# Softmax attentions with a fused bias-and-minimum instruction, row sums from a column of ones, and heads weighted together

## The chip, the cores and the metric

The kernel runs on one core of one Trainium2 chip. The metric is the device time of one execution of the whole program in microseconds; less is better.

## The reference

The program is one long network: three blocks of dense and attention layers over 256 positions of width 1024, all in fp32. The change touches only its softmax attentions, of which there are five: three branches of a sparse attention with 16 heads (two on causal rows, one on 15 compressed positions), a forgetting attention with 16 heads, and a block attention with 8 heads.

```python
# first_block, nsa: three branches share q; gates is a sigmoid per head and branch
s = einsum('qghd,ngd->ghqn', qi, kcb) - slopes * dist_c       # compressed, 15 positions
p_cmp = masked_softmax(s, dist_c >= 0, -1)
o_cmp = einsum('ghqn,ngd->qghd', p_cmp, vcb)
...                                                           # o_sel, o_win: the same on the causal rows
o = gb[..., 0:1] * o_cmp + gb[..., 1:2] * o_sel + gb[..., 2:3] * o_win

# second_block, fox_mix: forgetting attention
log_f = log_sigmoid(fz + fgate_b)
c = cumsum(log_f, axis=1)
logits = q @ k.T * FOX_HD ** -0.5 + c[q] - c[k]
probs = softmax(where(pos_q >= pos_k, logits, -inf))
out = probs @ v

# third_block, moba_attention: with 256 positions one causal block
p = softmax(where(mask, q @ k.T * dh ** -0.5, -1e30))
out = p @ v
```

## The kernel before, in words

The 256 positions are two tiles (`t`, `TT = 2`) of 128 partitions. The program is a list of stages. Each stage has a part for each engine, and unless a stage is "open" all four engines meet at a barrier at its end (`Chip.phase_end`: drain, increment `phase_done`, wait for all four). Dense stages (`SplitWeights` and what derives from it) stream weights from a ring of four 1 MB slots, split each half into a high and a low part (ScalarE L1116, VectorE L1124), and do three products for one. Attention stages use no weights.

A causal attention is made by `causal_attention` (L2402) as three stages:

- `Scores` (L2285). One job per tile and head: the product of 128 queries with the `n` keys that they can see (`n` is 128 for tile 0, 256 for tile 1) into one of four PSUM banks; VectorE adds the bias (`how`: distance times slope at L3565, decay and mask at L3523, scale and mask at L3689) and writes `p`; then `row_max` (L2331) takes the negated maximum of the row; ScalarE does the exponential with this as bias, in place, and its accumulator gives the row sum (L2350). TensorE waits for the bias instruction of four jobs ago before it fills a bank again. When all are done, VectorE waits for ScalarE's drain (L2351) and takes the reciprocals of the sums (L2344). In the compressed branch 32 multiplications with a mask come before that (L2343).
- `Gates` (L2520), in the sparse attention only: two small products of the reciprocals with the gates of the branch, in a stage of their own.
- `Turn` (L1532): transposes of `p` on TensorE, four to a bank, copied out by VectorE (L1566) and ScalarE (L1573) in turn.
- `Values` (L2354): products of the transposed weights with the values, 8 heads of 64 columns to a bank; VectorE scales each head by its own factor into `h_tok` (L2387), or scales and adds (L2385) in the second and the compressed branch. 8 or 16 heads of a tile are 8 or 16 instructions.

In the order of the program: projections, the causal branches 1 and 2, `Compress` (a small network on the keys and values), the compressed branch, then `Features` and `OutProj`. In the forgetting attention `ToNormedHeads` projects and norms, `ForgetGates.add_up` makes the cumulated decays `c` and `c_t` with five small products, `ToHeads` (L2539) brings queries and keys to feature order, and in it GpSimd issues 16 DMAs (L2563) that write one row of decays into each head's keys; `Scores` begins with a wait for them (`decays_landed`). The order in each engine is that of the program; nothing is planned by cost.

## Time and profile before

| | |
|---|---|
| median of 3 runs | 3816.76 us (3811.96 to 3827.05) |
| profiled execution | 3812.13 us, span 3810.3 us |
| TensorE busy | 3637.0 us (95%) |
| VectorE busy | 3061.5 us (80%) |
| ScalarE busy | 2060.6 us (54%) |
| GpSimd busy | 122.1 us (3%) |
| DMA | 744.52 MB, mean 195 GB/s |

Durations below come from the profiled execution. A duration in a timeline row runs from start to end of an instruction, and neighbours on one engine overlap, so the pace of an engine is read from start to start. "Idle before" says how long the engine stood and what ended it. A matrix product of fp32 operands shows as two rows. "ACTq", "DVEq" and "POOLq" are the queues of ScalarE, VectorE and GpSimd, as a barrier or a DMA issued there shows.

### The profile page before, as it was taken

To read this page: it belongs to the slowest core of one execution; us is meant where nothing else is said; L and a number is where in the kernel's file an instruction comes from. 1 tells how busy PE (TensorE), PEld (TensorE's weight loads), DVE (VectorE), ACT (ScalarE), POOL (GpSimd) and SP (SyncE) were. 2 spreads that over 40 slices of the span, in tenths; PEclk is the share of its full clock that TensorE was granted. 3 is DMA by queue.
4 is the path that set the end of the run, shared out by engine and by line. 5 is a ranking of instruction groups with operands and counts; after the bars stand their busy time and mean duration, and the time that the engine had idled before them with its cause. 6 is when DMAs were issued, how large, how long until landed. Compare 5 with 4: busy or idle time off the path is not lost. (4 is left out here: it accounts for less than half of the span.)

```text
span 3810.3 us, 59916 instructions
## 1 busy us (share of the span) xinstructions
PE 3637.0 (95%) x22328; PEld 3116.2 (82%) x22328; DVE 3061.5 (80%) x6382; ACT 2060.6 (54%) x4449; POOL 122.1 (3%) x112
## 2 busy tenths in 40 slices
PE   6999999999889979999999999999999999999898
PEld 5887788887778767998888887799988888888687
DVE  7887688887678776988888956689798997788766
ACT  3554555555355545545656456554555655555455
POOL 0000000000000000400000000050000000000000
PEclk9999999999789989999999999999999999999899
DMA  8767375766247523544454454254455545686354
GB/s 325 277 243 287 125 295 209 299 221 240 100 181 268 213 85 138 184 156 177 178 185 180 166 188 156 78 177 159 174 177 179 181 172 178 232 308 261 122 188 155
DMA packets 119619, 744.52 MB, mean 195 GB/s; under 512 B 13857, under 2 KB 14273, under 8 KB 44833
## 3 DMA queue, kind: packets, MB, share of 16 engines
q1 hardware_dynamic: 118082, 737.57, 52.9%
q8 instruction: 178, 2.92, 0.3%
q10 hardware_dynamic: 416, 2.06, 0.1%
q0 software_dynamic: 832, 1.06, 0.1%
q14 instruction: 111, 0.91, 0.1%
HBM read 738.53 MB, written 1.05 MB: 194 GB/s over the span
## 5 line engine op out<-in xcount | busy, mean ns | idle before, releaser
L212 PE MATMUL bank<-h_split,weights_high 128*128 128x512 f32 (+1 forms) x5824 | 1714.7, 358 | 15.5 <-DVE h_split L723 9.4
L1116 ACT ACTIVATE weights_high<-weight_ring 128x512 fp32r<-128x512 f32 x2248 | 1292.6, 624 | 650.9 <-PE bank L212 377.1
L1124 DVE TENSOR_TENSOR weights_low<-weight_ring,weights_high 128x512 fp32r<-128x512 f32 x2168 | 1394.9, 687 | 274.5 <-ACT weights_high L1116 252.9
L212 PE MATMUL bank<-h_split,weights_low 128*128 128x256 f32 x4800 | 1269.2, 280 | 0.0
L212 PEld LDWEIGHTS bank<-h_split,weights_high 128*128 128x128 f32 x5824 | 1014.8, 189 | 163.4 <-issue 16.7
L212 PEld LDWEIGHTS bank<-h_split,weights_low 128*128 128x128 f32 x4800 | 911.1, 190 | 37.8
L212 PE MATMUL acc<-weights_high,hidden_high 128*128 128x512 f32 x1552 | 613.8, 395 | 2.6 <-DVE hidden_low L1298 2.4
L212 PE MATMUL acc<-weights_high,hidden_low 128*128 128x512 f32 x1552 | 605.0, 390 | 0.0
L212 PE MATMUL acc<-weights_low,hidden_high 128*128 128x512 f32 x1552 | 604.5, 390 | 0.0
L212 PEld LDWEIGHTS acc<-weights_high,hidden_low 128*128 128x128 f32 x1552 | 291.3, 188 | 63.9
L212 PEld LDWEIGHTS acc<-weights_low,hidden_high 128*128 128x128 f32 x1552 | 291.7, 188 | 59.8 <-issue 0.2
L212 PEld LDWEIGHTS acc<-weights_high,hidden_high 128*128 128x128 f32 x1552 | 291.3, 188 | 56.2 <-issue 4.2
L1263 ACT ACTIVATE work<-bank 128x256 f32<-128x256 f32 x264 | 101.8, 386 | 344.9 <-PE bank L212 344.9
L212 PE MATMUL bank<-weights_high,h_split 128*128 128x512 f32 x704 | 222.8, 395 | 7.4 <-DVEq L234 2.9
L212 PEld LDWEIGHTS bank<-weights_high,h_split 128*128 128x128 f32 x704 | 133.6, 190 | 38.8 <-DVEq L234 3.9
L2249 DVE TENSOR_TENSOR h_tok<-h_feat,work 128x2048 f16<-128x2048 f16 x128 | 156.0, 1219 | 0.0
L2169 ACT ACTIVATE work<-bank 128x256 f32<-128x256 f32 x128 | 49.2, 384 | 193.2 <-PE bank L212 193.2
L212 PE MATMUL bank<-work 128*128 128x64 f32 (+10 forms) x896 | 125.6, 333 | 19.5 <-ACTq L234 8.3
L212 PE MATMUL bank<-weights_low,h_split 128*128 128x512 f32 x352 | 138.3, 393 | 0.0
L212 PEld LDWEIGHTS bank<-work 128*128 128x128 f32 (+5 forms) x896 | 108.0, 213 | 35.4 <-ACTq L234 11.1
L2171 ACT ACTIVATE work<-bank 128x256 f32<-128x256 f32 x128 | 49.3, 385 | 141.2 <-PE bank L212 141.2
L348 DVE SCALAR_TENSOR_TENSOR mod_sums<-h_tok,columns,mod_sums 128x512 f32<-128x512 f32 x160 | 112.5, 746 | 15.5 <-DMA h_tok<-slots 14.8
(347 smaller groups left out, 3522.1 us busy)
## 6 DMA issues: line engine op xcount, KB each, us to landing
weight_ring<-stream SPq DMA_DIRECT2D x574, 1024.0 KB, 4.8
h_feat<-slots SPq DMA_DIRECT2D x96, 512.0 KB, 5.8
h_tok<-slots SPq DMA_DIRECT2D x94, 512.0 KB, 5.9
work<-slots SPq DMA_DIRECT2D x26, 512.0 KB, 8.4
mod_sums<-biases SPq DMA_DIRECT2D x7, 1536.0 KB
h_feat<-rows SPq DMA_DIRECT2D x8, 512.0 KB, 3.8
work<-rows SPq DMA_DIRECT2D x7, 512.0 KB, 4.7
work<-biases SPq DMA_DIRECT2D x1, 1536.0 KB
```

The costliest lines, as they stand in the source:

```text
L212: ins = self.nc.tensor.matmul(out, lhs, rhs, start=start, stop=stop)
L348: ins = dve.scalar_tensor_tensor(self.sums.where[:, a], k.buffers[self.buffer][:, h * BANK:(h + 1) * BANK], c, self.sums.where[:, a], ALU. ...
L1116: act.activation(k.w_hi[:, b, q * self.QUARTER:(q + 1) * self.QUARTER], self.raw(g, q), ACT.Copy).then_inc(k.highs_ready, 1)
L1124: return eng.tensor_tensor(k.w_lo[:, b, w], self.raw(g, q), k.w_hi[:, b, w].bitcast(F32), ALU.subtract)
L1263: act.activation(self.rests[:, part, :], self.bank_of(c, part)[:, S:2 * S], ACT.Copy).then_inc(k.scalar_for_vector.sem, k.scalar_for_vecto ...
L2169: act.activation(self.place(c), k.bank[:, c % 2, 0:S], ACT.Gelu).then_inc(k.hidden_made, 1)
L2171: act.activation(self.place(c), k.bank[:, c % 2, S:2 * S], ACT.Copy).then_inc(k.hidden_rests, 1)
L2249: dve.tensor_tensor(cut(hot2), grid(self.places, N_KEYS), spread(self.pairs[:, S + b * BATCH:S + (b + 1) * BATCH, :], N_KEYS), ALU.is_equal)
```

## The change

- In `Scores` VectorE does one `tensor_tensor_reduce` per job: `p = (scores + bias) * scale` with a negative scale, and the minimum of `p` over the row into `low`. Sign and slope move into the constants and the scale; for the sparse attention the slope is divided out of the queries beforehand (`steep`, a factor for each feature column instead of a number). ScalarE takes the exponential of `-p + low` without an accumulator. A dummy exponential stands at the head of ScalarE's part.
- The values have a 65th column of ones for each head (`VW`), written by GpSimd in the first `Scores`, so that the product in `Values` also gives the row sum. Keys with a mask of the compressed branch are set to zero by two multiplications in place of 32.
- `Values` fills banks with at most 7 heads of 65 columns (16 heads: 5, 5 and 6), takes the reciprocals of the sums, multiplies them with the gates (where there are gates; the stage `Gates` is gone) and weights all heads of a bank in one instruction with a broadcast factor. In the second and the compressed branch the result goes to `parts` and GpSimd adds it to `h_tok`. All fills have a bank of their own, in `bank` and `acc`.
- In the forgetting attention the decay of the query row, the same for a whole row of scores, is no longer added; three of the five small products in `add_up` and one copy go. GpSimd issues the 16 DMAs of the key decays in `ToNormedHeads` (`hand_out`), when VectorE has made them and ScalarE has cleared the places, and no more in `ToHeads`.

The core of the diff (the rest: semaphores, the copies into 65-wide places, and the passing of arguments):

```diff
-    out["dist"] = np.where(tok >= q[None, None, :], tok - q[None, None, :], 1e32).reshape(P, -1)
+    out["dist"] = np.where(tok >= q[None, None, :], q[None, None, :] - tok, -1e32).reshape(P, -1)
...
-    out["cmp_dist"] = np.where(d >= 0, d, 1e32).reshape(P, -1)
+    out["cmp_dist"] = np.where(d >= 0, -d, -1e32).reshape(P, -1)
     out["cmp_mask"] = (d >= 0).reshape(P, -1)
+    out["steep"] = HD ** -0.5 / nsa_slope(2 * np.arange(DC)[None, :] + p[:, None] // HD)
...
@@ -2292,6 +2312,8 @@
 
     def gpsimd(self, pool):
         k = self.k
+        if self.ones is not None:
...
@@ -2306,9 +2328,10 @@
 
 
 
-    def __init__(self, k, jobs, top, total, keep=None, decays=0):
+    def __init__(self, k, jobs, low, keep=(), decays=0, ones=None):
         super().__init__(k)
-        self.jobs, self.top, self.total, self.keep, self.decays = jobs, top, total, keep, decays
+        self.jobs, self.low, self.keep, self.decays, self.ones = jobs, low, keep, decays, ones
+        self.scored = k.scored.reserve(len(jobs))
 
     def tensor(self, pe):
         k = self.k
@@ -2316,77 +2339,93 @@
             pe.wait_ge(k.decays_landed, 16 * self.decays)
         for i, (product, n, how, p) in enumerate(self.jobs):
             if i >= NB:
-                pe.wait_ge(k.vector_for_tensor.sem, k.vector_for_tensor.take())
+                pe.wait_ge(k.scored.sem, self.scored + i - NB + 1)
             product(k.bank[:, i % NB, 0:n]).then_inc(k.banks_for_vector.sem, k.banks_for_vector.send())
-        k.vector_for_tensor.skip(NB)
 
     def vector(self, dve):
         k = self.k
-        n_jobs = len(self.jobs)
-        begun = []
-
-        def row_max(i):
-            n, p = self.jobs[i][1], self.jobs[i][3]
-            dve.wait_ge(k.vector_for_tensor.sem, begun[i])
-            dve.tensor_reduce(self.top[:, i:i + 1], p, AX, ALU.max, negate=True).then_inc(k.vector_for_scalar.sem, k.vector_for_scalar.send())
-
+        for i, (product, n, (bias, scale), p) in enumerate(self.jobs):
+            dve.wait_ge(k.banks_for_vector.sem, k.banks_for_vector.take())
+            dve.tensor_tensor_reduce(p, k.bank[:, i % NB, 0:n], bias, scale, 3e38, ALU.add, ALU.min,
+                                     accum_out=self.low[:, i:i + 1]).then_inc(k.scored.sem, 1)
+        for p, keep in self.keep:
+            dve.wait_ge(k.scalar_for_vector.sem, k.scalar_for_vector.take())
+            dve.tensor_tensor(p, p, keep, ALU.mult)
+
+    def scalar(self, act):
+        k = self.k
+        act.activation(k.small[:, 88:89], k.small[:, ONES:ONES + 1], ACT.Exp)
+        per = len(self.jobs) // max(1, len(self.keep))
         for i, (product, n, how, p) in enumerate(self.jobs):
+            act.wait_ge(k.scored.sem, self.scored + i + 1)
+            ins = act.activation(p, p, ACT.Exp, scale=-1.0, bias=self.low[:, i:i + 1])
+            if self.keep and i % per == per - 1:
+                ins.then_inc(k.scalar_for_vector.sem, k.scalar_for_vector.send())
+
+
+class Values(Stage):
+
+
+
+    def __init__(self, k, heads, jobs, out, total, gates=None, parts=None, floor=False):
+        super().__init__(k)
+        self.heads, self.jobs, self.out, self.total = heads, jobs, out, total
+        self.gates, self.parts, self.floor = gates, parts, floor
+        n = -(-heads // (BANK // VW))
+        cuts = [heads * i // n for i in range(n + 1)]
+        self.fills = [(t, a, b) for t in range(TT) for a, b in zip(cuts, cuts[1:])]
+        self.weighted = k.weighted.reserve(len(self.fills)) if parts is not None else None
+
+    def bank(self, f):
+        return self.k.bank[:, f, :] if f < NB else self.k.acc[:, f - NB, :]
+
+    def tensor(self, pe):
+        k = self.k
+        for f, (t, a, b) in enumerate(self.fills):
+            for h in range(a, b):
+                p_t, v = self.jobs[t * self.heads + h]
+                for i, (lhs, rhs) in enumerate(zip(p_t, v)):
+                    mm = k.mm(self.bank(f)[:, (h - a) * VW:(h - a + 1) * VW], lhs, rhs, start=i == 0,
+                              stop=i == len(v) - 1, last=True)
+            mm.then_inc(k.banks_for_vector.sem, k.banks_for_vector.send())
+
+    def result(self, f):
+        t, a, b = self.fills[f]
+        return self.out[:, t, a * HD:b * HD].rearrange("p (h d) -> p h d", d=HD)
+
+    def part(self, f):
+        t, a, b = self.fills[f]
+        at = (t * self.heads + a) * HD
+        return self.parts[:, at:at + (b - a) * HD].rearrange("p (h d) -> p h d", d=HD)
+
+    def vector(self, dve):
+        k = self.k
+        for f, (t, a, b) in enumerate(self.fills):
             dve.wait_ge(k.banks_for_vector.sem, k.banks_for_vector.take())
-            how(dve, p, k.bank[:, i % NB, 0:n]).then_inc(k.vector_for_tensor.sem, k.vector_for_tensor.send())
-            begun.append(k.vector_for_tensor.sent)
-            if i >= 1:
-                row_max(i - 1)
-        row_max(n_jobs - 1)
-        dve.wait_ge(k.scalar_for_vector.sem, k.scalar_for_vector.take())
-        if self.keep is not None:
-            for i, (product, n, how, p) in enumerate(self.jobs):
-                ins = dve.tensor_tensor(p, p, self.keep(i), ALU.mult)
-        dve.reciprocal(self.total[:, 0:n_jobs], self.total[:, 0:n_jobs])
-
-    def scalar(self, act):
-        k = self.k
-        for i, (product, n, how, p) in enumerate(self.jobs):
-            act.wait_ge(k.vector_for_scalar.sem, k.vector_for_scalar.take())
-            act.activation(p, p, ACT.Exp, bias=self.top[:, i:i + 1], accum_out=self.total[:, i:i + 1])
-        act.drain().then_inc(k.scalar_for_vector.sem, k.scalar_for_vector.send())
-
-
-class Values(Stage):
-
-
-
-    def __init__(self, k, jobs, add, width=64):
-        super().__init__(k)
-        self.jobs, self.add, self.w = jobs, add, width
-        self.per = BANK // width
-
-    def tensor(self, pe):
-        k = self.k
-        for i, (p_t, v, factor, out) in enumerate(self.jobs):
-            f, j = i // self.per, i % self.per
-            if j == 0 and f >= NB:
-                pe.wait_ge(k.vector_for_tensor.sem, k.vector_for_tensor.take())
-            for a, (lhs, rhs) in enumerate(zip(p_t, v)):
-                mm = k.mm(k.bank[:, f % NB, j * self.w:(j + 1) * self.w], lhs, rhs, start=a == 0,
-                          stop=a == len(v) - 1, last=True)
-            if j == self.per - 1:
-                mm.then_inc(k.banks_for_vector.sem, k.banks_for_vector.send())
-        fills = len(self.jobs) // self.per
-        k.vector_for_tensor.skip(min(NB, fills))
-
-    def vector(self, dve):
-        k = self.k
-        for i, (p_t, v, factor, out) in enumerate(self.jobs):
-            f, j = i // self.per, i % self.per
-            if j == 0:
-                dve.wait_ge(k.banks_for_vector.sem, k.banks_for_vector.take())
-            src = k.bank[:, f % NB, j * self.w:(j + 1) * self.w]
-            if self.add:
-                ins = dve.scalar_tensor_tensor(out, src, factor, out, ALU.mult, ALU.add)
-            else:
-                ins = dve.tensor_scalar(out, src, factor, None, ALU.mult)
-            if j == self.per - 1:
-                ins.then_inc(k.vector_for_tensor.sem, k.vector_for_tensor.send())
+            src = self.bank(f)[:, 0:(b - a) * VW].rearrange("p (h d) -> p h d", d=VW)
+            total = self.total[:, t * self.heads + a:t * self.heads + b]
+            sums = src[:, :, HD]
+            if self.floor:
+                dve.tensor_scalar(total, sums, 0.5, None, ALU.max).then_inc(k.dve_step, 1)
+                dve.wait_ge(k.dve_step, k.step("dve"))
+                sums = total
+            dve.reciprocal(total, sums).then_inc(k.dve_step, 1)
+            dve.wait_ge(k.dve_step, k.step("dve"))
+            if self.gates is not None:
+                dve.tensor_tensor(total, total, self.gates[:, t, a:b], ALU.mult).then_inc(k.dve_step, 1)
+                dve.wait_ge(k.dve_step, k.step("dve"))
+            dst = self.result(f) if self.parts is None else self.part(f)
+            ins = dve.tensor_tensor(dst, src[:, :, 0:HD], total.unsqueeze(2).to_broadcast([P, b - a, HD]), ALU.mult)
+            if self.parts is not None:
+                ins.then_inc(k.weighted.sem, 1)
+
+    def gpsimd(self, pool):
+        k = self.k
+        if self.parts is None:
+            return
+        for f in range(len(self.fills)):
+            pool.wait_ge(k.weighted.sem, self.weighted + f + 1)
+            pool.tensor_tensor(self.result(f), self.result(f), self.part(f), ALU.add)
 
 
 def weight_blocks(p0, p1, heads):
...
@@ -2556,13 +2578,6 @@
                 ins = eng.tensor_copy(dst, half) if parity == 0 else eng.activation(dst, half, ACT.Copy)
             ins.then_inc(sent.sem, sent.send())
 
-    def gpsimd(self, pool):
-        k = self.k
-        for h in range(FOX_HEADS):
-            key = self.dst[HD:HD + 1, DC + h // 2, :] if h % 2 == 0 else self.odd[1][0:1, h // 2, :]
-            pool.dma_start(key, self.decays[h:h + 1, :]).then_inc(k.decays_landed, 16)
-
-
 class ToNormedHeads(ToTokens):
 
...
-            for a in range(t + 1):
-                k.mm(k.acc[:, 3, t * H:(t + 1) * H], tri[:, a, t * P:(t + 1) * P], self.lf[:, a, :],
-                     start=a == 0, stop=a == t, last=True)
         for a in range(TT):
             mm = k.mm(k.acc[0:H, 2, 0:S], self.lf[:, a, :], tri[:, a, :], start=a == 0, stop=a == TT - 1, last=True)
         mm.then_inc(k.banks_for_vector.sem, k.banks_for_vector.send())
...
+            dve.tensor_scalar(self.c_t, k.acc[0:H, 2, 0:S], -1.0, None, ALU.mult).then_inc(k.decays_made, 1)
+
+    def hand_out(self, pool):
+
+        k = self.k
+        pool.wait_ge(k.decays_made, 1)
+        pool.wait_ge(k.heads_cleared, 2)
+        for h in range(FOX_HEADS):
+            key = self.even[HD:HD + 1, DC + h // 2, :] if h % 2 == 0 else self.odd[1][0:1, h // 2, :]
+            pool.dma_start(key, self.c_t[h:h + 1, :]).then_inc(k.decays_landed, 16)
 
     def fill(self, act, dst, value):
         n, rows = dst.shape[0], dst.rearrange("p c (t q) -> p (c t) q", q=P)
...
 
     def how(t, h, n):
-        return lambda dve, dst, bank: dve.scalar_tensor_tensor(dst, bank, c[:, t, h:h + 1], mask[:, t, 0:n],
-                                                               ALU.add, ALU.add)
-
-    att = causal_attention(k, FOX_HEADS, side(0), side(DC), lambda h, a: v[:, a, h * HD:(h + 1) * HD], how, p, p_t,
-                           top, total, total, k.h_tok, False, decays=FOX_HEADS)
+        return mask[:, t, 0:n], -1.0
+
+    att = causal_attention(k, FOX_HEADS, side(0), side(DC), lambda h, a: v[:, a, h, :], how, p, p_t, low, total,
+                           k.h_tok, decays=FOX_HEADS, ones=v[:, :, :, HD])
     return out + att + [Features(k, k.h_tok), OutProj(k)]
 
...
+    projected = ToTokens(k, [(v[:, :, :, 0:HD], None)])
+    parts, branches = p.rearrange("p a b -> p (a b)"), gates.rearrange("p t (h b) -> p t h b", b=3)
     out = [head, features, projected]
     for branch in (1, 2):
         first = DC + 4 + 4 * (branch - 1)
         kt = lambda h, first=first: feat[64 * (h % 2):64 * (h % 2) + 64, first + h // 4, :]
-        val = lambda h, a, b=branch: v[:, a, (b - 1) * kv + h // 4 * HD:(b - 1) * kv + (h // 4 + 1) * HD]
-        att = causal_attention(k, H, q, kt, val, alibi(dist), p, p_t, top, total, factor, k.h_tok, branch == 2)
+        val = lambda h, a, b=branch: v[:, a, (b - 1) * NSA_GROUPS + h // 4, :]
+        att = causal_attention(k, H, q, kt, val, alibi(dist), p, p_t, low, total, k.h_tok,
+                               ones=v[:, :, :, HD] if branch == 1 else None, gates=branches[:, :, :, branch],
+                               parts=parts if branch == 2 else None)
         if branch == 1:
             att[0].copy_couples(feat[:, DC:DC + 4, :], couples)
-        out += [att[0], Gates(k, factor, gates, total, branch), att[1], att[2]]
```

## Rows read from the trace of the kernel before

**Rows 1.** Timeline of TensorE, sparse attention: start us, us, engine, line, operation, count, idle before.

```profile
931.46 0.71 PE L212 MATMUL bank<-work 64*128 64x128 f32 x8 [0.72 <-ACTq L234]
...
950.62 7.74 PE L1549 MATMUL bank<-constants,work 128*128 128x128 f32 x48 [3.68 <-DVEq L234]
959.08 10.93 PE L212 MATMUL bank<-work 128*128 128x64 f32 x96 [0.72 <-ACTq L234]
...
971.77 0.72 PE L212 MATMUL bank<-work 64*128 64x128 f32 x8 [1.76 <-DVEq L234]
...
990.93 8.06 PE L1549 MATMUL bank<-constants,work 128*128 128x128 f32 x48 [3.68 <-DVEq L234]
...
1039.14 7.34 PE L212 MATMUL bank<-work 64*128 64x15 f32 x64 [0.53 <-DVEq L234]
1054.56 5.20 PE L1549 MATMUL bank<-constants,work 128*15 128x128 f32 x32 [8.07 <-DVEq L234]
```

**Rows 2.** Timeline of TensorE, forgetting attention, from its scores to its transposes.

```profile
2379.29 0.79 PE L212 MATMUL bank<-work 65*128 65x128 f32 x2 [4.94 <-POOLq L234]
...
2382.01 0.63 PE L212 MATMUL bank<-work 65*128 65x128 f32 x2
2382.44 0.63 PE L212 MATMUL bank<-h_feat,work 128*128 128x128 f32 x2
...
2400.36 8.19 PE L1549 MATMUL bank<-constants,work 128*128 128x128 f32 x48 [4.05 <-DVEq L234]
```

**Rows 3.** Timeline of TensorE, third block's attention.

```profile
3547.85 0.71 PE L212 MATMUL bank<-work 64*128 64x128 f32 x8 [0.72 <-ACTq L234]
...
3558.12 5.26 PE L1549 MATMUL bank<-constants,work 128*128 128x128 f32 x24 [3.72 <-DVEq L234]
```

**Rows 4.** Timeline of VectorE, scores of the first causal branch.

```profile
937.73 0.27 DVE L3565 SCALAR_TENSOR_TENSOR work<-constants,bank 128x128 f32<-128x128 f32 x1
937.92 0.28 DVE L2331 TENSOR_REDUCE work<-work 128x1 f32<-128x128 f32 x1
...
938.67 0.41 DVE L3565 SCALAR_TENSOR_TENSOR work<-constants,bank 128x256 f32<-128x256 f32 x1
939.00 0.41 DVE L2331 TENSOR_REDUCE work<-work 128x1 f32<-128x256 f32 x1
```

**Rows 5.** Timeline of ScalarE in the same scores.

```profile
939.89 0.39 ACT L2350 ACTIVATE work<-work 128x128 f32<-128x128 f32 x1
940.19 0.19 ACT L2350 ACTIVATION_READ_ACCUMULATOR work<-work 128x1 f32 x1
940.28 0.49 ACT L2350 ACTIVATE work<-work 128x256 f32<-128x256 f32 x1
940.68 0.19 ACT L2350 ACTIVATION_READ_ACCUMULATOR work<-work 128x1 f32 x1
```

**Rows 6.** The same view of ScalarE: its first row in these scores.

```profile
932.81 1.28 ACT L2350 ACT_TABLE_LOAD   x1 [1.44 <-DVE work L2331]
```

**Rows 7.** Line 626: an operation, its count, then ns least/median/most, starts, shape.

```profile
L626 DVE DVE_READ_ACCUMULATOR x_tok<-x_tok,h_tok x12: 80/82/84, 234.1 to 1299.1; 128x1 f32 x12
```

**Rows 8.** Windows: stretch, its us, busy time (rows) of each engine, clock, DMA share, GB/s.

```profile
959.00:965.00 6.00, 5.92 (x53) 5.92 (x54) 3.25 (x16) 0.00 (x0) 0.00 (x0) 1.00 0.01 3
...
978.00:984.00 6.00, 6.00 (x23) 4.91 (x21) 6.00 (x21) 5.44 (x21) 0.00 (x0) 0.50 0.00 0
```

**Rows 9.** Timeline of TensorE's weight loads, second causal branch.

```profile
980.77 0.50 PEld L212 LDWEIGHTS bank<-work 64*128 64x128 f32 x2 [0.16 <-DVE work L3565]
```

**Rows 10.** Timelines of VectorE and of GpSimd at the end of ToHeads.

```profile
2375.35 0.69 DVE L2556 COPY h_feat<-bank 64x512 f32<-64x512 f32 x1
...
2377.06 0.49 POOL L2563 DMA_DIRECT2D h_feat<-work  x1
```

**Rows 11.** Timeline of VectorE, last fill of the first branch's values.

```profile
970.05 1.62 DVE L2387 TENSOR_SCALAR h_tok<-bank,work 128x64 f32<-128x64 f32 x8 [1.95 <-PE bank L212]
```

**Rows 12.** Groups of GpSimd by form, whole span: busy us, mean ns, idle before.

```profile
L1124 POOL TENSOR_TENSOR weights_low<-weight_ring,weights_high 128x512 fp32r<-128x512 f32 x80 | 103.8, 1321 | 361.2 <-ACT weights_high L1116 361.2
```

116 lines of the change are left out of this document (63 added, 53 removed).

## The prediction

> **What bounds the kernel now.** I read the page first: TensorE is busy for 95% of the span and VectorE for 80%. The span is a chain of dense stages (weight splitting and products) in which TensorE sets the time, and nothing in the change touches those, so the share of busy time says little here. The second view is the timeline of TensorE around the attention stages, because there it stops. Each softmax attention is three stages with a barrier of all four engines between them: `Scores`, `Turn`, `Values`. Rows 1 give their starts in the sparse attention: scores from 931.46, transposes from 950.62; scores from 971.77, transposes from 990.93; compressed scores from 1039.14, transposes from 1054.56. Every one of these transposes begins after 3.7 to 8.1 us of idle TensorE. `Scores` takes 19.16, 19.16 and 15.42 us. The other two are 21.07 us (2379.29 to 2400.36) [rows 2] and, with 8 heads, 10.27 us (3547.85 to 3558.12) [rows 3].
>
> What sets the 19.16 is read from the timelines of VectorE and ScalarE in the same stretch. VectorE does two instructions for each head, back to back: for a 128-wide block they follow each other at 0.19 to 0.20 us, for a 256-wide one at 0.33 [rows 4]. So a head costs 0.39 or 0.66 us, 16 of each cost 16.8 us. ScalarE needs 0.30 or 0.40 for the exponential and 0.09 for reading its row sum [rows 5], 0.39 and 0.49, or 14.1 us: it mostly waits for VectorE. It also loads its exponential table for 1.28 us only after the first minimum has come [rows 6]. After the last exponential the reciprocal and, in the sparse attention, the gates follow on VectorE, and only then the barrier opens.
>
> **Part by part.** (a) *The fused instruction.* It replaces two VectorE instructions by one that also writes a row minimum. The trace has no such instruction. The nearest is the one at L626, a three-operand instruction with an accumulator: it is shown as the main instruction and a read of the accumulator of 0.082 us [rows 7]. With 0.01 for the gap between them, the fused pace is 0.20 + 0.09 = 0.29 and 0.33 + 0.09 = 0.42 us, so 16 x 0.29 + 16 x 0.42 = 11.3 us. Its bounds: below, the read costs nothing, 0.20 and 0.33 (8.5 us); above, it is as dear as the two instructions it replaces, 0.39 and 0.66 (16.8 us). I take 0.29 and 0.42, since L626 has the same pieces.
>
> (b) *ScalarE without row sums.* The exponential keeps its bias in a column, so 0.30 and 0.40 stay and the 0.09 goes [rows 5]: 16 x 0.30 + 16 x 0.40 = 11.2 us, for 8 heads of each width 5.6, and for the compressed scores (15 wide, by the slope between the two widths 0.21) 32 x 0.21 = 6.7. VectorE at 11.3 and ScalarE at 11.2 are then in balance; whichever it is, the stage costs 11.3. The dummy exponential at the head of the stage moves the table load under the first products: the first useful one starts 1.28 + 0.2 = 1.5 us after the stage, or, where the table is there already, after the first product and the first fused instruction (0.9, an estimate: 0.7 for the first four products, of which it needs one, and 0.29). The reciprocals and gates leave `Scores`, so the tail after the last exponential is 0.2.
>
> (c) *TensorE under it.* It must now deliver a score block every 0.3 to 0.4 us. Between 978 and 984 the granted clock was 0.50, that is the 1.2 GHz level [rows 8], and there the weight loads of one 256-wide head took 0.50 us, behind which TensorE waited 0.16 for VectorE [rows 9]. At this level 0.50 is more than 0.42: 16 x 0.08 = 1.3 us are lost in the second branch and, as the first branch has the low clock for part of its length, 0.5 there. In the forgetting attention at low clock a 128-wide head costs 0.43 (2382.01 to 2382.44) [rows 2] against 0.29, and the clock there was low after TensorE had stood for 4.94 us; this wait goes (below), so I put 1.0 us for a part of it.
>
> (d) *Sum over the score stages.* First branch 1.5 + 11.3 + 0.2 + 0.5 = 13.5, from 19.16: 5.7. Second 0.9 + 11.3 + 0.2 + 1.3 = 13.7: 5.5. Compressed: 1.5 + 6.7 + 0.2, and 0.6 for the one mask multiplication of 240 columns (0.41 by the 256-wide row [rows 4], and its wait) that follows the last exponential in place of 16 of the 32 small ones: 9.0 from 15.42, 6.4. Forgetting: 1.5 + 11.3 + 0.2 + 1.0 = 14.0 from 21.07: 7.1. The last one: 1.5 + 5.7 + 0.2 = 7.4 from 10.27: 2.9. Together 27.6 us.
>
> (e) *Decay rows handed out earlier.* GpSimd issues 16 DMAs in `ToHeads`, the last at 2377.06 for 0.49 us, and TensorE waits until 2379.29 for them. VectorE's last copy of that stage ends at 2376.04 [rows 2, 10]. In the new place they are issued in the stage before, from the point where VectorE has made the rows (`g == 17` of 24 weight halves, so six halves of dense products and the whole of `ToHeads` still lie ahead). So scores start at 2376.15: 3.1 us. Sixteen issues at 0.49 are 7.8 us, which six halves of 48 products cover, and if they were twice as dear they would reach past the end of that stage by little. GpSimd's barrier is the only thing queued behind them. The Trainium skill (SBUF — State Buffer, Who interferes with whom) says that a VectorE instruction with two SBUF inputs contends with GpSimd's reads, and VectorE splits weights that way in the new place; by it the issues could stretch, and by the doubled bound just given that is at most 1 us.
>
> (f) *Three small matrix products fewer* in `add_up`, on a TensorE that is busy without a gap there. They have 16 columns; three heads of the forgetting scores with 128 columns cost 1.3 us even at the low clock [rows 2], so this is worth well under that. I count nothing and let the range hold it.
>
> (g) *Values.* The products have 65 columns for 64; if the time went with the columns, the 10.9 us [rows 1] would grow by 0.2 per causal stage, if by the weight load, by nothing; I count nothing. Before, 8 instructions of 0.2 us follow the last product: 970.05 to 971.67, and TensorE starts again at 971.77 [rows 1, 11]. Now one reciprocal (0.16), one gate product (0.16) where there are gates, and one instruction over 6 heads, 384 columns, 0.55 by the slope of rows 4, with two or three waits of 0.03 on its own result: 0.8 or 1.0 us. So 0.7 is saved in branch one, 0.9 in the forgetting attention, 1.0 in the last one (4 heads, 0.42): 2.6. In branch two and in the compressed branch GpSimd adds each part behind that. Its 512-wide sum took 1.32 us [rows 12], 384 columns are 1.0 us, plus the 0.16 for the floor in the compressed one: these tails grow by 0.3 and 0.5, -0.8 in sum. GpSimd keeps up before the last fill, since a fill takes TensorE 2 us or more. Net 1.8. The Trainium skill (Vector Engine (DVE) Microarchitecture Reference, Measured stream behaviour on trn2) gives 1.30 ns instead of 1.05 for a column where pairs of words start on an odd word; a row of 65 words makes every second head start so. By it the last weighting of each stage would be some 0.1 us longer, five times, half a microsecond; the copies into the values are under TensorE's products. No row here has such a layout.
>
> (h) *At nothing:* column factors for the query scale, 8 instructions on each of ScalarE and VectorE under TensorE's dense products (without that cover under 1 us); the ones, written by GpSimd during `Scores`, where it only has four DMA issues; the DMA stream, because the score stages move almost nothing ([rows 8] has 0 GB/s) and the weight ring is full long before.
>
> The sum is 27.6 + 3.1 + 1.8 = 32.5 us. The profiled execution took 3812.1 us (span 3810.3), so 3779.6. The median of the runs shown is 4.6 us above the profiled one; the after is measured as a median too, so I forecast 3784.
>
> **The rivals.** *A: the fused instruction costs as much as the pair.* Then VectorE paces as before, 16.8 us instead of 11.3 in three stages, 8.4 for 5.7 in the short one: 19.2 us of the gain are gone, less about 2.8 because TensorE's low clock no longer costs. What stays is the tails, the decays, the compressed scores and `Values`, 16.1 us: 3801. For it speaks that the trace has no such instruction; against it L626.
>
> *B: the clock takes the gain.* `Turn` and `Values` now run on a TensorE that has worked faster before, or come in another phase. Causal `Values` ran at the 2.4 GHz level, 96 rows in 10.93 us [rows 1, 8]. If the clock fell to 1.2 GHz in them, at up to twice the time, three of them cost 2 x 10.9 + 8.3, up to 30 us. That is the far bound; one of them falling costs 11: 3794. Against it speaks that the transposes before them are unchanged and now follow a shorter idle. The same rival has a good side: forgetting scores without any low clock, and the compressed `Values` too, give 3 to 5 us more: 3778.
>
> *C, on the other side: the fused instruction is slower than the pair.* All of the 32.5 us are gone when each of the 144 costs 0.23 us more than I took: 0.65 for a 256-wide one and 0.52 for a 128-wide one, which is about two unfused instructions with nothing overlapping (0.82 and 0.56 by their durations [rows 4]). At these durations the three 16-head stages cost 22.1 us each instead of 11.3, the short one 5.4 more, the compressed one some 4: 41.8 us, time 3825, slower than before by 0.2%. Above 0.37 us extra it is slower by over 0.5%. No row supports it but the absence of the instruction.
>
> *D: the hidden waits.* The change does what it says on the engines, but the end of each stage was covered by a transfer. Against it: DMA moved nothing in these stretches. It would give 3812.
>
> **How the numbers follow.** Forecast (3770 to 3792, with B's good side and one clock phase) 0.68; A and mixtures with it (3792 to 3806) 0.16; B's bad side 0.08; C 0.05, of which 0.02 slower by over 0.5%; D 0.03. The runs of before spread from 3812 to 3827, so a median of the after may lie 5 us to each side. The range is 3768 to 3802: it leaves out D, C, some of A and of B, and runs that are fast by more than I allow, together some 0.2. Half a percent is 19 us, about what a measurement of this kernel can tell from no change; it puts the border at 3798. Faster by more: the forecast, most of B and a quarter of A, 0.79. Within: 0.19. Slower: 0.02.
>
> **What would show it.** Right: VectorE starts one fused instruction every 0.29 and 0.42 us, with a small accumulator read behind each; ScalarE's reads of row sums are gone; the stages take 13 to 14 us from TensorE's first score row to the first transpose; no wait for GpSimd's queue ahead of the forgetting scores; GpSimd rows of about 1 us at the end of branch two and of the compressed branch. Wrong: fused rows of 0.4 us or more for 128 columns (A or C), granted clock of 0.50 in the causal `Values` (B), or TensorE waiting for a DMA behind a shortened stage (D).

## The result and the profile after

The changed kernel took 3768.84 us (median of four executions, 3767.23 to 3775.98) beside 3814.52 us for the kernel before (four, 3811.96 to 3827.05): a ratio of 0.9879 with the 95% interval 0.9854 to 0.9905, 1.2% faster. The forecast was 3784 with a range of 3768 to 3802, so the median lies 0.8 us above the lower end of the range. The gain between the medians is 45.7 us, for a sum of 32.5 in the prediction. The profiled execution was the longest of its four, 3775.98 us with a span of 3773.8, so the two traces differ by 36.5 us.

The timeline of TensorE in the sparse attention answers to [rows 1]. Score stages start at 931.71, 964.88 and 1022.12, transposes at 944.34, 977.64 and 1030.69.

```profile
931.71 0.71 PE L216 MATMUL bank<-work 64*128 64x128 f32 x8 [0.72 <-ACTq L238]
...
944.34 7.78 PE L1569 MATMUL bank<-constants,work 128*128 128x128 f32 x48 [3.30 <-ACTq L238]
952.84 6.02 PE L216 MATMUL bank<-work 128*128 128x65 f32 x52 [0.72 <-ACTq L238]
...
964.88 0.71 PE L216 MATMUL bank<-work 64*128 64x128 f32 x8 [1.11 <-DVEq L238]
...
977.64 5.46 PE L1569 MATMUL bank<-constants,work 128*128 128x128 f32 x48 [1.73 <-ACTq L238]
983.82 6.02 PE L216 MATMUL bank<-work 128*128 128x65 f32 x52 [0.72 <-ACTq L238]
...
1022.12 7.42 PE L216 MATMUL bank<-work 64*128 64x15 f32 x64 [0.53 <-DVEq L238]
1030.69 5.49 PE L1569 MATMUL bank<-constants,work 128*15 128x128 f32 x32 [1.15 <-DVEq L238]
...
1049.22 1.12 PE L832 MATMUL bank<-constants,h_tok 128*128 128x128 f32 x4 [2.39 <-POOLq L238]
```

The same view of the forgetting attention and of the third block's, for [rows 2] and [rows 3]:

```profile
2352.13 0.80 PE L216 MATMUL bank<-work 65*128 65x128 f32 x2 [1.79 <-DVEq L238]
...
2353.15 0.64 PE L216 MATMUL bank<-work 65*128 65x128 f32 x2
2353.58 0.63 PE L216 MATMUL bank<-h_feat,work 128*128 128x128 f32 x2
...
2360.29 0.60 PE L216 MATMUL bank<-h_feat,work 128*128 128x256 f32 x2
2360.72 0.59 PE L216 MATMUL bank<-work 65*128 65x256 f32 x2
...
2367.17 5.46 PE L1569 MATMUL bank<-constants,work 128*128 128x128 f32 x48 [1.09 <-ACTq L238]
2373.35 9.06 PE L216 MATMUL bank<-work 128*128 128x65 f32 x52 [0.72 <-ACTq L238]
2382.21 9.59 PE L216 MATMUL acc<-work 128*128 128x65 f32 x44
2392.72 3.67 PE L832 MATMUL bank<-constants,h_tok 128*128 128x128 f32 x16 [0.91 <-DVEq L238]
```

```profile
3518.97 0.71 PE L216 MATMUL bank<-work 64*128 64x128 f32 x8 [0.72 <-ACTq L238]
...
3526.08 4.51 PE L1569 MATMUL bank<-constants,work 128*128 128x128 f32 x24 [2.30 <-ACTq L238]
3531.30 5.57 PE L216 MATMUL bank<-work 128*128 128x65 f32 x48 [0.72 <-ACTq L238]
3543.82 1.54 PE L832 MATMUL bank<-constants,h_tok 128*128 128x128 f32 x6 [6.95 <-DVEq L238]
```

Inside the first score stage, first VectorE (for [rows 4]), then ScalarE (for [rows 5] and [rows 6]):

```profile
932.57 0.08 DVE L2349 DVE_READ_ACCUMULATOR2_ANT work<- 128x1 f32 x1
932.57 0.29 DVE L2349 CUSTOM_DVE_ANT_0 work<-bank,constants 128x128 f32<-128x128 f32 x1
932.78 0.29 DVE L2349 CUSTOM_DVE_ANT_0 work<-bank,constants 128x128 f32<-128x128 f32 x1
...
936.42 0.42 DVE L2349 CUSTOM_DVE_ANT_0 work<-bank,constants 128x256 f32<-128x256 f32 x1
936.77 0.42 DVE L2349 CUSTOM_DVE_ANT_0 work<-bank,constants 128x256 f32<-128x256 f32 x1
```

```profile
931.72 1.28 ACT L2357 ACT_TABLE_LOAD   x1
...
933.13 11.14 ACT L2361 ACTIVATE work<-work 128x128 f32<-128x128 f32 x32
```

Fused instructions follow each other at 0.21 and 0.35 us; their accumulator reads of 0.08 start together with the next instruction. ScalarE runs 32 exponentials without a gap in 11.14 us. The stage is 1.42 us until the first exponential, 11.14 and 0.07 behind it, 12.63 us, and ScalarE sets it.

The Values of the forgetting attention took 19.37 us, where the kernel before took 12.70. The windows of the transposes and of these Values (columns as in [rows 8]) name the reason: the same 96 products (97 rows) ran at the 1.2 GHz level for most of the stage, the transposes before them wholly at 2.4.

```profile
2367.17:2373.35 6.18, 5.46 (x48) 5.22 (x48) 4.15 (x6) 3.59 (x6) 0.00 (x0) 1.00 0.01 3
2373.35:2392.72 19.37, 18.46 (x97) 18.27 (x97) 4.25 (x12) 0.03 (x1) 0.00 (x0) 0.57 0.00 0
```

**Where the 36.5 us lie.** Each entry is a difference of starts in the TensorE timelines, before minus after, in us; branch 2's Values end, and `Compress` begins, at VectorE's first copy of `Compress`. The last column is for a second trace of the changed kernel (the first experiment).

| | forecast | this trace | second trace |
|---|---|---|---|
| five score stages | 27.6 | 29.0 | 30.6 |
| wait for the decays | 3.1 | 3.15 | 3.1 |
| five transposes | 0 | 5.8 | 7.8 |
| five Values | 1.8 | -2.9 | 4.8 |
| `Compress` | 0 | 1.4 | 1.6 |
| everything else | 0 | 0.1 | 1.4 |
| sum | 32.5 | 36.5 | 49.3 |

Of the 1.4 us in `Compress`, 1.0 is the clock again: its last 20 products took 2.93 us at a granted clock of 0.50 before and 1.96 at 0.80 after (1.70 in the second trace).

### The profile page after: what moved, and what is told of

Read it like the earlier page. It is cut to its first block and busy times, and to the rows that moved or that the text cites. A ratio compares the mean times of both kernels' runs of the same rounds, so it can differ in the third digit from the quotient of the medians.

```text
span 3773.8 us, 59656 instructions
## 1 busy us (share of the span) xinstructions
PE 3616.3 (96%) x22322; PEld 3106.1 (82%) x22322; DVE 3027.5 (80%) x6276; ACT 2047.2 (54%) x4310; POOL 133.2 (4%) x128
## 3 DMA queue, kind: packets, MB, share of 16 engines
HBM read 738.54 MB, written 1.05 MB: 196 GB/s over the span
## 5 line engine op out<-in xcount | busy, mean ns | idle before, releaser
L216 PE MATMUL acc<-weights_high,h_split 128*128 128x512 f32 x384 | 122.0, 396 | 0.3 <-DVE weights_low L1135 0.3
L1135 POOL TENSOR_TENSOR weights_low<-weight_ring,weights_high 128x512 fp32r<-128x512 f32 x80 | 103.8, 1320 | 357.2 <-ACT weights_high L1127 357.0
```

The source lines that it names most:

```text
L216: ins = self.nc.tensor.matmul(out, lhs, rhs, start=start, stop=stop)
L1135: return eng.tensor_tensor(k.w_lo[:, b, w], self.raw(g, q), k.w_hi[:, b, w].bitcast(F32), ALU.subtract)
```

## The experiments

The theory that the trace suggests: ScalarE now sets the score stages, TensorE does so where its clock is low, and the stages behind gain or lose by the clock. All edits are to the changed kernel, and "more" and "less" are against its second trace. A median is of 4 to 10 executions, the stages are of one of them; the profiled one can lie some microseconds from the median. The stage times that they gave, in us, as starts in the TensorE timelines (order: branch 1, branch 2, compressed, forgetting, third block):

| kernel | median | scores | transposes | forgetting Values |
|---|---|---|---|---|
| before | 3814.5 | 19.16 19.16 15.42 21.07 10.27 | 8.46 8.78 5.91 8.91 5.98 | 12.70 |
| changed, first trace | 3768.8 | 12.63 12.76 8.57 15.04 7.11 | 8.50 6.18 6.20 6.18 5.22 | 19.37 |
| changed, second trace | 3771.1 | 12.63 12.72 8.58 13.49 7.11 | 7.85 6.19 6.46 6.18 3.56 | 11.85 |
| pair | 3797.6 | 18.17 18.17 8.72 19.05 9.76 | 9.08 8.23 5.87 8.40 5.89 | 11.85 |
| rowsum | 3794.4 | 15.59 15.17 10.88 15.36 8.59 | 8.95 7.84 5.79 8.85 6.10 | 11.84 |
| both | 3796.5 | 18.36 18.36 11.05 18.74 9.95 | 8.55 7.86 7.11 8.85 5.55 | 11.84 |
| late | 3778.4 | 12.63 12.73 8.58 15.17 7.11 | 8.76 6.18 6.29 6.18 3.56 | 19.23 |
| nopre | 3780.7 | 13.55 12.73 9.26 14.99 8.01 | 8.96 6.18 5.88 6.18 6.11 | 19.42 |
| heads | 3779.8 | 12.63 12.97 8.58 13.49 7.11 | 8.47 7.85 6.09 6.18 3.56 | 12.53 |
| lastadd | 3767.1 | 12.63 12.78 8.58 12.25 7.11 | 9.07 6.18 6.14 6.18 5.23 | 11.84 |
| busy | 3776.0 | 14.54 15.65 8.58 17.45 9.33 | 6.19 6.18 6.08 6.18 3.55 | 11.84 |
| best | 3773.8 | 12.64 12.97 8.58 12.25 7.11 | 7.77 6.18 6.72 6.18 5.18 | 11.84 |
| tail6 | 3773.6 | 12.63 13.74 8.58 15.01 7.49 | 6.18 6.18 6.38 6.18 3.55 | 19.39 |

### again: the changed kernel, unaltered

> The changed kernel once more, nothing altered. In its first trace the second-to-last attention's Values ran at granted clock 0.50 from 2376 us on and took 19.4 us, 6.7 more than before the change; that execution took 3775.98 us, its three others 3767.2 to 3769.7. Theory 1 (the low clock there is an accident of that execution): this trace shows clock 1.00 in those Values, 12.7 us, and a span near 3766. Theory 2 (the faster score stage brings it about every time): again 19 us and clock 0.50 there, and a span near 3773; then the 6 to 9 us between the executions lie elsewhere. The ratio to the kernel before: 0.988 by both.

Ratio 0.9882 (0.9842 to 0.9922), four executions: 3763.18, 3765.36, 3776.87, 3777.29 us. The first was profiled, with a span of 3761.0. Timeline of TensorE and window of the forgetting Values:

```profile
2371.12 6.02 PE L216 MATMUL bank<-work 128*128 128x65 f32 x52 [0.72 <-ACTq L238]
2376.98 5.08 PE L216 MATMUL acc<-work 128*128 128x65 f32 x44
```

```profile
2371.12:2382.97 11.85, 10.94 (x97) 10.80 (x97) 4.25 (x12) 0.03 (x1) 0.00 (x0) 1.00 0.00 0
```

The same instructions took 11.85 us here and 19.37 there, so theory 1: it belongs to the execution and not to the kernel. The mean granted clock separates the eight executions of this kernel in the same way: 0.976 or 0.977 in the five of 3763 to 3770 us, 0.972 or 0.973 in the three of 3776.0 to 3777.3.

### pair: the fused instruction undone

```diff
-            dve.tensor_tensor_reduce(p, bank, bias, scale, 3e38, ALU.add, ALU.min, accum_out=low)
+            dve.scalar_tensor_tensor(p, a, scale, b, ALU.mult, ALU.subtract)
...
+            dve.tensor_reduce(low, p, AX, ALU.min)     # one head behind
```

The arguments are shortened here. The slope is no more divided out of the queries but comes with the scale, and TensorE waits for the first of the two instructions before it fills a bank again.

> Only the fused instruction is undone: the bias instruction and the row minimum are two VectorE instructions again, everything else stays as changed (no row sums on ScalarE, table loaded ahead, heads weighted together). Theory 1 (VectorE's instruction count was what the score stages waited for): VectorE paces again at 0.39 and 0.66 us a head, 16.8 us for 16 heads of each width, so branch 1 takes 17.8 us for 12.6, branch 2 17.5 for 12.8, forgetting 17.8 for 15.0, third block 10.1 for 7.1, compressed 9.0 for 8.6: 16 us more than the change, about 3785, ratio to before 0.992. Theory 2 (ScalarE's row-sum reads were what the stages waited for and their removal brings the gain): the pair costs at most 3 us, about 3772, 0.989.

Ratio 0.9957 (0.9939 to 0.9974), 3797.64 us. VectorE in branch 1, two instructions a head:

```profile
941.36 0.41 DVE L2360 SCALAR_TENSOR_TENSOR work<-constants,bank 128x256 f32<-128x256 f32 x1
941.69 0.41 DVE L2354 TENSOR_REDUCE work<-work 128x1 f32<-128x256 f32 x1
```

The next pair began at 942.02, so the pace is 0.66 again, as in [rows 4]. The span grew by 27.9 us (3788.9 to 3761.0), more than theory 1's 16. The table splits it: the five score stages are 19.3 us longer (73.9 to 54.5), which is the 19.2 that rival A put on them, and the five transposes 7.2 us longer (37.5 to 30.2), though nothing in them was changed. Their granted clock fell: in branch 2 to 0.74 from 1.00, in the forgetting attention to 0.73 from 1.00. So theory 1 holds for the stages, and its sum left out what the transposes lose.

### rowsum: ScalarE's row sum read put back

```diff
-            ins = act.activation(p, p, ACT.Exp, scale=-1.0, bias=self.low[:, i:i + 1])
+            ins = act.activation(p, p, ACT.Exp, scale=-1.0, bias=self.low[:, i:i + 1],
+                                 accum_out=self.sums[:, i:i + 1])
```

> The changed kernel, but the exponential on ScalarE writes its row sum to a column again, which nothing reads. Theory 1 (with the fused instruction at 0.21 and 0.345 us, ScalarE at 0.30 and 0.40 is what the score stages wait for wherever TensorE is at full clock): the read of 0.09 comes on top, 2.9 us in branch 1, 2.0 in branch 2, 1.0 in the forgetting attention (there TensorE needs 0.43 a head), 1.4 in the third block, 1.6 in the compressed branch: 9 us more than the change, about 3778. Theory 2 (VectorE is the limit as in the forecast, 0.29 and 0.42): 0.39 and 0.49 on ScalarE against 0.29 and 0.42 gives 2.7, 2.0, 1.0, 1.3, so nearly the same sum, but the trace would show ScalarE waiting for VectorE in the change and not here. Theory 3 (TensorE is the limit in all of them): no more than 2 us.

Ratio 0.9939 (0.9918 to 0.9959), 3794.39 us. ScalarE in branch 1:

```profile
942.27 0.49 ACT L2361 ACTIVATE work<-work 128x256 f32<-128x256 f32 x1
942.67 0.18 ACT L2361 ACTIVATION_READ_ACCUMULATOR work<-work 128x1 f32 x1
942.76 0.49 ACT L2361 ACTIVATE work<-work 128x256 f32<-128x256 f32 x1
```

The pace is 0.49 for 0.40, and branch 1 is 2.96 us longer, as theory 1 has it: a read of 0.09 us on ScalarE is on the path of 32 heads. The score stages grew by 11.1 us (theory 1: 8.9). But the time grew by 23 to 26 us. The trace has it behind the score stages: transposes 7.3 us, branch 2's Values with `Compress` 46.9 us for 38.1 at a mean granted clock of 0.71 for 0.90 (47.2 us in both, but 38.8 in pair), the third block's Values 2.5 (granted clock 0.59). So most of what rowsum loses is clock. In the changed kernel ScalarE didn't wait for VectorE in branch 1 (32 exponentials without a gap), so theory 2 falls.

### both: pair and rowsum together

The edit is the two above.

> Both halves of the score stage undone: bias and row minimum as two VectorE instructions (as in pair), and the exponential writes its row sum again (as in rowsum; nothing reads it). The early decays, the table load ahead and the heads weighted together stay. Theory 1 (a stage takes what its slowest engine takes, so that the two undone parts don't add up): VectorE's 0.39 and 0.66 us cover ScalarE's 0.39 and 0.49, the score stages are those of pair (18.2, 18.2, 19.1, 9.8 us), the time is pair's, about 3798; the remaining 14 us to the kernel before are decays, table load and Values. Theory 2 (the two add up): 28 + 25 us more than the change, 3822, slower than before.

Ratio 0.9953 (0.9937 to 0.9969), 3796.54 us: theory 1. Undone alone, pair costs 27 to 29 us and rowsum 23 to 26 (against the two medians of the changed kernel); undone together they cost 25 to 28. The score stages are those of pair but for 2.6 us, most of them in the compressed branch. So taking the row sums from ScalarE while VectorE still does two instructions is worth 2.6 us there. The other half alone is not nothing: from both to rowsum the score stages are 10.9 us shorter (76.5 to 65.6), and from both to the changed kernel 21.9 (to 54.5). The two traces' spans differ likewise, 3799.3 to 3790.2; the medians only by 2.2 us, with executions spread over 10 and 20 us. What is left beside the two halves is worth 3813.0 - 3796.5 = 16.5 us against the kernel before, measured beside it. By the traces 8.6 of it still lie in the score stages (85.1 to 76.5: table load, masks, and the reciprocals and gates that left them), the rest is the decays and Values.

### late: decays handed out in ToHeads again

```diff
 class ToHeads(ToFeatures):
+    def gpsimd(self, pool):
+        self.gates.hand_out(pool)
...
 class ToNormedHeads(ToTokens):
-    def gpsimd(self, pool):
-        self.gates.hand_out(pool)
```

> The changed kernel, but GpSimd issues the 16 decay rows in ToHeads again and no more in the stage before. Theory 1: TensorE stands 4.9 us instead of 1.8 before the first forgetting score, 3.1 us more than the change, about 3772, and nothing else moves. Theory 2 (the clock answers): the longer stand shifts the low-clock stretch, as in the kernel before, where the transposes paid for it (8.9 us for 6.2) and the Values after them ran at full clock; then against a changed kernel with slow Values it would be 0 to 4 us faster, against one with fast Values 6 us slower.

Ratio 0.9897 (0.9859 to 0.9934), 3778.42 us. TensorE's first forgetting score:

```profile
2357.11 0.80 PE L216 MATMUL bank<-work 65*128 65x128 f32 x2 [4.92 <-POOLq L238]
```

GpSimd's last issue began at 2354.89 and took 0.48. The wait is 4.92 us for 1.79: 3.1 us, as forecast, and theory 1 on the trace. The score stage started at the low clock in this trace and in the first one of the changed kernel alike, 15.17 and 15.04 us, so the low start comes with both waits. The median is 7 to 10 us above the changed kernel's two; its four executions, 3775.7 to 3781.1, have clocks of 0.973 and 0.974, like the slower ones of the changed kernel. Against those three the difference is 1 to 2 us, against the first trace (3775.5 to 3773.8) 1.7.

### nopre: no table load ahead

```diff
-        act.activation(k.small[:, 88:89], k.small[:, ONES:ONES + 1], ACT.Exp)
```

> The changed kernel without the dummy exponential at the head of each score stage, so the table load stands behind the first row minimum again. Theory 1 (the load is on the path at the head of each stage where the table isn't there): +1.1 us in branch 1, +1.1 in the third block, +1.0 in the forgetting attention, +1.2 in the compressed branch, nothing in branch 2: 4.4 us, plus what the transposes behind lose to the clock (0 to 4): ratio to before about 0.9895 to 0.990. Theory 2 (ScalarE has slack at the head and catches up): under 1 us.

Ratio 0.9908 (0.9883 to 0.9934), 3780.70 us. ScalarE in branch 1:

```profile
933.43 1.28 ACT L2360 ACT_TABLE_LOAD   x1 [1.10 <-DVE work L2349]
934.73 1.57 ACT L2360 ACTIVATE work<-work 128x128 f32<-128x128 f32 x5
```

Branch 1 is 0.92 us longer, compressed 0.68, third block 0.90, branch 2 nothing: 2.5 us where theory 1 had 3.4 for these. The forgetting stage is as in the first trace (14.99 to 15.04): there TensorE at the low clock lets ScalarE catch up, theory 2. The transposes of branch 1 and of the third block took 8.96 and 6.11 us beside 7.85 and 3.56, and the forgetting Values were the long ones (19.42 to 11.85). Against the first trace of the changed kernel, which has long Values too, the span is 4.6 us longer (3778.4 to 3773.8), and 2.5 of that is the table load. The 10 to 12 us between the medians are therefore mostly clock, and the run can't price the load by its median.

### heads: one weighting instruction for each head

```diff
-            ins = dve.tensor_tensor(dst, src[:, :, 0:HD], total.unsqueeze(2).to_broadcast(...), ALU.mult)
+            for i in range(b - a):
+                ins = dve.tensor_scalar(dst[:, i, :], src[:, i, 0:HD], total[:, i:i + 1], None, ALU.mult)
```

> The changed kernel, but each head of a bank is weighted by its own VectorE instruction from its own column (6 of 64 columns instead of one of 384). Theory 1 (only the last bank of a Values stage lies behind the last product): 6 x 0.2 = 1.2 us against 0.56, so +0.6 us a stage, five stages (four heads in the third block, +0.4): 3 us. Theory 2 (VectorE has so much slack in Values that the instruction count is hidden but for the last one): under 0.3 a stage. Theory 3 (VectorE can't keep up on the short banks of tile 0 either): over 1 us a stage, and TensorE waits inside Values.

Ratio 0.9910 (0.9882 to 0.9938), 3779.80 us. VectorE behind branch 1's last bank: six instructions in 1.24 us, where the changed kernel has one of 0.56.

```profile
964.22 1.24 DVE L2419 TENSOR_SCALAR h_tok<-acc,work 128x64 f32<-128x64 f32 x6
```

Values of branch 1, forgetting and third block: 12.73, 12.53, 12.95 us for 12.05, 11.85, 12.52, so +0.7, +0.7, +0.4, theory 1. The compressed Values took 15.10 us for 12.09. The length alone would not show much, since this stage took 14.44 us in best and 14.57 in both with no such edit, at a granted clock of 0.55 and 0.57 (0.69 in the second trace). But in heads VectorE worked without a gap from the first bank (1041.81) to the end of the last (1054.30), theory 3. Part of its work there is waiting for GpSimd: five of its six gate products took 0.63 to 0.76 us for 0.17 (last section). Where TensorE's products are single and short, weighting the heads together was worth 3 us in this trace and not 0.6.

### lastadd: VectorE adds the last part

```diff
+                if f == len(self.fills) - 1:
+                    dve.wait_ge(k.weighted.sem, self.weighted + f + 1)
+                    dve.tensor_tensor(self.result(f), self.result(f), self.part(f), ALU.add)
...
-        for f in range(len(self.fills)):
+        for f in range(len(self.fills) - 1):
```

> The changed kernel, but the last of the six parts in branch 2 and in the compressed branch is added by VectorE instead of GpSimd. Theory 1 (GpSimd's last addition, 0.99 us, is on the path of both stages): 0.55 us on VectorE instead, the compressed Values end 0.5 to 0.6 us earlier (11.6 for 12.1 to 12.3) and branch 2's too: 1 us. Theory 2 (VectorE and GpSimd get in each other's way: gate products took 0.68 and 0.82 us instead of 0.17 when an addition ran beside them): VectorE's own addition is stretched by GpSimd's one before, and nothing or less is gained. The median can't tell 1 us; the stages of the trace can.

Ratio 0.9875 (0.9849 to 0.9901), 3767.11 us: the fastest kernel of the study, and the difference to the changed one is within what can't be told apart. VectorE behind branch 2 in lastadd, and then GpSimd and VectorE at the same place in the changed kernel's second trace:

```profile
996.80 0.56 DVE L2418 TENSOR_TENSOR work<-acc,work 128x384 f32<-128x384 f32 x1
997.39 0.56 DVE L2423 TENSOR_TENSOR h_tok<-h_tok,work 128x384 f32<-128x384 f32 x1
998.14 0.38 DVE L2527 COPY work<-weight_ring 128x416 f32<-128x416 f32 x1 [0.19 <-POOLq L238]
```

```profile
994.64 0.56 DVE L2419 TENSOR_TENSOR work<-acc,work 128x384 f32<-128x384 f32 x1
...
996.35 0.38 DVE L2525 COPY work<-weight_ring 128x416 f32<-128x416 f32 x1 [1.15 <-POOLq L238]
```

```profile
995.28 0.99 POOL L2429 TENSOR_TENSOR h_tok<-h_tok,work 128x384 f32<-128x384 f32 x1 [1.89 <-DVE work L2419]
```

From the last weighting to the next stage: 1.34 us for 1.71, and 1.24 for 1.74 in the compressed branch (1049.78 to 1051.02, 1046.73 to 1048.47). That is 0.9 us, theory 1. GpSimd's addition before it was over when VectorE's began. The compressed Values as a whole ended only 0.2 us earlier (11.90 for 12.09), since the last bank's weighting came later.

### busy: TensorE kept working through the score stages

```diff
+            if n == S and i % 2 and not self.decays:
+                product(k.acc[:, 3, 0:n])
+        if n == S:
+            for i in range(len(self.jobs) - NB, len(self.jobs)):
+                pe.wait_ge(k.scored.sem, self.scored + i + 1)
+                product(k.acc[:, 3, 0:n])
+                product(k.acc[:, 3, 0:n])
```

> The changed kernel with extra products that nothing reads, into a PSUM bank that is free here: in the causal score stages of the sparse and the third attention one after every second 256-wide head, and in all causal score stages two behind each of the last four fused instructions, so that TensorE doesn't stand while the last exponentials run. Nothing is left out. Theory 1 (the transposes and Values run at granted clock 0.5 for a part because TensorE stood and waited in the score stage before them): branch 1's transposes take 6.2 us instead of 7.9 to 8.8, the third block's 3.6 every time instead of 3.6 to 5.2, the forgetting Values 11.9 us every time instead of 11.9 or 19.4; the score stages grow by at most 0.5 each. Median about 3764, its runs within 5 us of each other instead of 14. Theory 2 (the clock's low stretches come whatever TensorE does in these stages): the same two groups of runs as before, 3763 to 3768 and 3776 to 3777, plus 1 to 2 us for the longer score stages.

Ratio 0.9898 (0.9871 to 0.9924), 3775.98 us. TensorE in the third block, from the extra products to the transposes:

```profile
3521.09 4.04 PE L216 MATMUL acc<-work 64*128 64x256 f32 x18
3525.22 2.84 PE L1569 MATMUL bank<-constants,work 128*128 128x128 f32 x24
```

The clock part of theory 1 held: transposes 6.19, 6.18, 6.18 and 3.55 us, granted clock 1.00 in each, and forgetting Values of 11.84. Its price was wrong: an extra product took 0.43 us and they weren't hidden, so the causal score stages grew by 1.9 to 4.0 us, 11.0 in all. The executions lie 6 us apart (3772.8 to 3779.2) instead of 14. For branch 1 the filling decides at which level the transposes run: they took 6.2 us in the two kernels that fill the gap before them (busy, tail6) and 7.8 to 9.1 in the other eleven traces. So theory 2 falls there. The third block proves less, since again, late and heads have 3.56 us without any filling. The median is 12 us above theory 1's 3764.

### best and tail6: only the last gap filled

```diff
+        if n == S:
+            for i in range(1 if self.decays else 3):     # tail6: 2 and 6
+                product(k.acc[:, 3, 0:n])
```

Both have lastadd's edit too.

> The changed kernel with VectorE adding the last part of branch 2 and of the compressed branch (as in lastadd), and with products that nothing reads behind the last score of each causal stage: three of 0.43 us where TensorE stood 1.7 to 3.3 us (sparse branches, third block), one in the forgetting attention, where it stood 1.1. No extra product elsewhere, and no wait. Nothing is left out. Theory 1 (it is enough that TensorE stands less in the tail): score stages stay at 12.6, 12.7 and 7.1, transposes of branch 1 take 6.2 us instead of 7.9 to 9.1, of the third block 3.6 instead of 3.6 to 5.2, no slow forgetting Values; median 3762, under lastadd's 3767. Theory 2 (what kept the clock up in the busy kernel was a TensorE without any gap): the transposes are as in lastadd, 9.0 and 5.2 us, and the median is lastadd's, 3767.

> As best, with six extra products (2.6 us) for three and two for one, so that TensorE works until about the end of the last exponential. Theory 1: the same clock as in best, branch 2's score stage 0.9 and the third block's 0.3 us longer: 1 us slower than best. Theory 2 (no gap at all is needed): only here do the transposes fall to 6.2 and 3.6 us; 3763 against best's 3767.

Ratios 0.9906 (0.9882 to 0.9929) and 0.9903 (0.9880 to 0.9926), 3773.81 and 3773.64 us. In best the transposes of branch 1 and of the third block stayed at 7.77 and 5.18 us; in tail6 they fell to 6.18 and 3.55. So theory 2 for branch 1: three products leave TensorE standing for 1.1 us before the transposes and don't keep the clock up, six (0.7 us) do; for the third block it fits too, with the doubt named above. Branch 2 doesn't need it: its transposes run at 2.4 GHz after 1.7 us of standing. Tail6's forgetting Values took 19.39 us, behind transposes that had run wholly at 2.4 GHz, as in late and nopre, which fill nothing. Neither median beat lastadd's (forecast: 3762 and 3763), so filling the gaps before the transposes was not worth its price.

## Why the prediction was right, and where it wasn't

**What bounds the score stages (a, b).** The step that failed in the stages is the size of the fused instruction. It was put at 0.29 and 0.42 us because the accumulator read at L626 [rows 7] was laid end to end with the main instruction. The trace has 0.21 and 0.35: the lower bound of the prediction (0.20 and 0.33) was nearly right, because the read runs beside the next instruction. At L626 the instruction behind a read starts 0.11 us after it (234.12 to 234.23), and there are only twelve, never one behind another; that row couldn't price a stream. It changed little, since ScalarE's 11.2 us stood in the sum as the twin of VectorE's 11.3, and ScalarE did take 11.14. rowsum shows that it is the limit.

**TensorE's share (c).** Branch 2 lost 0.6 us for the 1.3 forecast (first to last exponential 11.7 us for 11.1). In the compressed scores TensorE (7.42 us busy at clock 0.50 in 8.57) and ScalarE (7.09 us for its exponentials, 6.7 forecast) were nearly even, and step (d) had only ScalarE; their table was loaded before the stage began, so the first exponential came after 0.96 us and not 1.5. 9.0 was forecast for 8.57. In the forgetting attention 128-wide heads took the 0.43 us of [rows 2], for seven of the stage's fifteen microseconds. What was missed there is the 256-wide head: 0.43 us too, at 2.4 GHz (2360.29 to 2360.72, granted clock 1.00), more than ScalarE's 0.40. The 64-row heads of the other stages come two in 0.43 us: in busy, two of them and one extra product took 0.86 (936.33 to 937.19). Stage 15.0 or 13.5 us, forecast 14.0.

**The stages (d).** 12.6, 12.8, 8.6, 15.0, 7.1 for a forecast of 13.5, 13.7, 9.0, 14.0, 7.4: 29.0 us for 27.6, all within 1.1.

**Decays (e).** 3.15 us for 3.1. The 16 issues took 7.7 us in the new place as well (first at 2331.59, last at 2338.79 for 0.49), and TensorE's wait is for VectorE's queue now. They were not stretched beside VectorE's weight splitting: 0.48 to 0.51 us each, as in late, where nothing is split.

**Values (g).** Without the clock, the tails gained 0.65 in branch 1 (0.7 forecast), 0.85 in the forgetting attention (0.9; second trace), 1.0 in the third block (16.26 - 12.52, of which 8.31 - 5.57 are the products' clock; 1.0), and lost 0.31 (0.3) in branch 2 and 0.1 to 0.35 (0.5) in the compressed one. The 65th column cost nothing: 96 products in 10.93 us as in [rows 1]. The last weighting took 0.56 us for 384 columns (0.55 forecast), GpSimd's addition 0.99 (1.0). The Trainium skill (Vector Engine (DVE) Microarchitecture Reference, Measured stream behaviour on trn2) and its 1.30 ns a column for pairs that start on an odd word didn't show: the weighting of 256, 320 and 384 columns took 0.424, 0.491 and 0.558 us, 1.05 ns a column. The Trainium skill's row is for odd starts on both sources; here one source has them, rows of 65 words in PSUM, and the other is a broadcast factor.

**The clock (rival B).** This is the term that was mis-sized, on both sides, and it is the main reason why the median came out 15 us under the forecast. The bad side happened in the profiled execution: one causal Values at 1.2 GHz, 7.5 us more than at 2.4 (19.37 to 11.85) where 11 was forecast. The good side was looked for in the wrong place. The prediction left `Turn` out of the sum with the words that its transposes "are unchanged and now follow a shorter idle", and drew from that only that they wouldn't get worse. They ran 5.8 and 7.8 us faster than before in the two traces, branch 2 and forgetting at clock 1.00 where they had 0.69 and 0.68, and the third block's Values gained another 2.7. No trace lies near the median of 3769: the two are of 3776.0 and 3763.2 us. In the second the gain is 16.8 us above the sum (49.3 to 32.5). Of that 7.8 are the transposes, 2.7 the third block's Values and 1.2 `Compress`, 11.7 us of clock in all; 3.0 are the score stages. The 4.6 us that were added to get from the profiled execution to the median were too much as well: the median of four before is 3814.5, 2.4 above the profiled one. That the number still fell into the range owes something to luck: the good side of B was put at 3 to 5 us, and more than twice that came.

**Rivals A, C, D.** A is refuted by the pace in the trace, and pair shows what it would have cost: 19.3 us in the score stages, as A had it, but 28 in all, because the slower stages give the transposes' clock away too. C fell with the pace. D: no transfer ended late behind a stage; all of the 36.5 us arrive in the span.

**What stays open.** Why the forgetting Values fall to 1.2 GHz in one execution and not in the next. In all four traces where they did (the first of the changed kernel, late, nopre, tail6), the score stage before had a mean granted clock of 0.77 or 0.78 and took 15.0 to 15.2 us; where it had 0.87 and took 13.49 (again, heads), or 1.00 and 12.25 (lastadd, best), they stayed at 2.4 GHz. But low scores aren't enough. Busy, with its extra products, had 0.81 there, and pair 0.77, and their Values ran at 2.4 GHz; in pair the transposes had been low instead (0.73). No run here forces the one or the other.
